# Attention values: a wide matmul over both parts of the weights, and a sum in two halves

## The chip, the cores and the metric

The kernel runs on one core of one Trainium2 chip. The metric is device microseconds from the start to the end of one execution; lower is better. TensorE multiplies, ScalarE and VectorE do the element-wise work, GpSimd helps at a few places, and the SP queue issues the weight transfers.

## The reference, cut to what matters

Two transformer stacks run one after the other on 256 tokens of width 1024, in fp32. Two of their layers have attention: the second layer of the first stack (called layer 0 of the attention in the kernel) and the layer of the second stack (layer 1). The part that the change touches is the projection to queries, keys and values:

```
z = h @ w_in
qkv = z[..., :3 * ATT_W].reshape(bsz, s, 3, H_ATT, HEAD_DIM).transpose(2, 0, 3, 1, 4)
q, k, v = qkv[0], qkv[1], qkv[2]
...
xn = rmsnorm_2(h, g_attn[i])
proj = xn @ w_in[i]
sb_q, sb_k, sb_v, d_q, d_k, d_v = jnp.split(proj, offsets, axis=-1)
```

Values are then weighed by softmax probabilities (layer 0: forgetting and block attention; layer 1: differential attention, then stick-breaking attention).

## The kernel before

**Precision.** Every large product is made of three fp32r products: x and the weights are each split into a high part (rounded to fp32r) and a low part (what is left), and high·high, low·high and high·low are summed in PSUM. ScalarE rounds the weights (line 578, `wh`), VectorE or GpSimd subtracts (lines 974 and 516, `wl`).

**Units.** Weights come in units of 1024 columns of 128 partitions, four to a quad, each in a slot of a ring of four (`raw`, `wh`, `wl`, each `[P, RING, SLOT]`). A semaphore `lo_ready[s]` tells TensorE that a slot is split. Queries and keys are made with the weights as the stationary operand and x moving (`unit`, lines 1556 to 1558): 24 matmuls of 256 columns. Values are wanted with tokens on the partitions, so there x is stationary and the weights move (`value_unit`, lines 1679 to 1682).

**The projection of a layer.** It has 24 units, u = 0 to 23, in four groups g of six: query and key of one head pair (u%6 = 0, 1), two units that together hold the values of two pairs (2, 3), and query and key of the next pair (4, 5). The head pairs are taken in turns j = 0 to 9; in turn j TensorE works through units 3j, 3j+1 and 3j+2, and between them `scores(j-1)`, `turn(j-1)` (transposes of the probabilities, line 1767) and `weigh(j-2)` (probabilities times values, lines 1792 and 1794). The order is written out by hand for each engine. An engine takes its instructions in order.

**Banks.** The projection has three PSUM banks (0 to 2). `bank_free(u)` holds TensorE until the unit that last used the bank has been read. Queries and keys are read by VectorE (`read_out`, line 1295, semaphore `bank_read`), values by ScalarE (`read_values`, line 823, semaphore `values_read`). Both values halves (tokens 0 to 127 and 128 to 255) share one bank. Scores are in banks 3 and 4, transposed probabilities in banks 5 and 6 (`turned_banks`), the output in bank 7.

**VectorE's turn j** is, in order: `logits(j-1)` (line 1319), `read_out(3j)`, the split of unit 3j+3 (`split_next(3j-1)`), `normalise(j-1)` (lines 1334 to 1351), `read_out(3j+1)` in the first two turns, the split of unit 3j+4, the low part of an output, later turns' `read_out(3j+1)`, the split of unit 3j+5 and `read_out(3j+2)`. In layer 1 the first turn also has one reciprocal (line 1465), after which GpSimd scales h (lines 561 and 562) beside the next turns. ScalarE's turn has the softmax exponentials (line 798), the rounding of a unit (line 578), then in odd turns `read_values`.

## Time and profile before

| | |
|---|---|
| time, three runs | 906.71 us median (906.47 to 907.17) |
| the profiled execution | 907.1 us, span 905.4 us |
| TensorE matmuls | 898.6 us busy, 99% of the span |
| VectorE, ScalarE, GpSimd busy | 670.1, 572.1, 243.6 us |
| granted TensorE clock | 0.999 |
| chain that ended last | TensorE 95%, VectorE 2%, ScalarE 1% |

The span runs from the first to the last instruction of the profiled execution; 1.7 us of its time lie outside the span. A matmul's busy time overlaps that of the next, so that how fast TensorE goes is read from the starts of successive matmuls and not from their durations.

### The profile page before, as it was taken

To read this page: it belongs to the slowest core of one execution; us is meant where nothing else is said; L and a number is where in the kernel's file an instruction comes from. 1 tells how busy PE (TensorE), PEld (TensorE's weight loads), DVE (VectorE), ACT (ScalarE), POOL (GpSimd) and SP (SyncE) were. 2 spreads that over 40 slices of the span, in tenths; PEclk is the share of its full clock that TensorE was granted. 3 is DMA by queue.
4 is the path that set the end of the run, shared out by engine and by line. 5 is a ranking of instruction groups with operands and counts; after the bars stand their busy time and mean duration, and the time that the engine had idled before them with its cause. 6 is when DMAs were issued, how large, how long until landed. Compare 5 with 4: busy or idle time off the path is not lost.

```text
span 905.4 us, 18274 instructions
## 1 busy us (share of the span) xinstructions
PE 898.6 (99%) x6022; PEld 814.0 (90%) x6022; DVE 670.1 (74%) x1353; ACT 572.1 (63%) x996; POOL 243.6 (27%) x130
## 2 busy tenths in 40 slices
PE   9999999999999999999999999999999999999997
PEld 8999888888898999988888888999998888888897
DVE  8987887786657756678777866788667766686566
ACT  7456776774445556577666644667658877774453
POOL 0421444420000002044443000070104988850000
PEclk9999999999999999999999999999999999999999
DMA  8545677677534434456666654444335655576521
GB/s 307 196 167 163 210 236 238 210 225 268 173 130 140 139 129 153 162 167 210 231 193 212 230 190 147 127 154 141 119 122 179 211 190 192 192 236 208 185 96 47
DMA packets 47193, 163.51 MB, mean 181 GB/s; under 512 B 5234, under 2 KB 10098, under 8 KB 47141
## 3 DMA queue, kind: packets, MB, share of 16 engines
q1 hardware_dynamic: 42336, 158.12, 53.5%
q10 hardware_dynamic: 4805, 4.70, 1.6%
q8 instruction: 32, 0.52, 0.3%
q14 instruction: 20, 0.16, 0.1%
HBM read 161.71 MB, written 3.44 MB: 182 GB/s over the span
## 4 chain that ended last, share of the span: by engine, by line
PE 95%; DVE 2%; ACT 1%; issue 1%; DVEq 0%
PE psum L1532 41%; PE psum L1533 20%; PE psum L1556 7%; PE psum L1557 7%; PE psum L1558 7%; PE psum L1679 2%; PE psum L1681 2%; PE psum L1682 2%; PE psum L1792 1%; PE psum L1894 1%; PE psum L1767 1%; PE psum L1731 1%; PE psum L1729 1%; ACT wh L578 1%; PE psum L1905 0%
## 5 line engine op out<-in xcount | busy, mean ns | idle before, releaser
L578 ACT ACTIVATE wh<-raw 128x1024 fp32r<-128x1024 f32 (+2 forms) x266 | 297.1, 1119 | 116.4 <-PE psum L1533 80.6
L1532 PE MATMUL psum<-xs,wh 128*128 128x512 f32 x1056 | 367.2, 394 | 0.0
L516 POOL TENSOR_TENSOR wl<-raw,wh 128x1024 fp32r<-128x1024 f32 (+1 forms) x86 | 209.5, 2440 | 450.7 <-ACT wh L578 449.3
L1533 PE MATMUL psum<-xs,wl 128*128 128x256 f32 x1056 | 292.7, 277 | 0.0
L974 DVE TENSOR_TENSOR wl<-raw,wh 128x1024 fp32r<-128x1024 f32 (+2 forms) x180 | 241.3, 1345 | 52.3 <-ACT wh L578 52.0
L1532 PEld LDWEIGHTS psum<-xs,wh 128*128 128x128 f32 x1056 | 198.0, 188 | 45.9
L1533 PEld LDWEIGHTS psum<-xs,wl 128*128 128x128 f32 x1056 | 198.3, 188 | 0.1
L1532 PE MATMUL psum<-ys,wh 128*128 128x512 f32 x528 | 183.2, 394 | 0.0
L1533 PE MATMUL psum<-ys,wl 128*128 128x256 f32 x528 | 146.3, 277 | 0.0
L1556 PE MATMUL psum<-xs,wh 128*128 128x256 f32 x416 | 120.3, 289 | 0.0
L1532 PEld LDWEIGHTS psum<-ys,wh 128*128 128x128 f32 x528 | 99.0, 188 | 23.0
L1558 PE MATMUL psum<-xs,wl 128*128 128x256 f32 x416 | 117.6, 283 | 0.0
L1557 PE MATMUL psum<-xs,wh 128*128 128x256 f32 x416 | 117.6, 283 | 0.0
L1031 DVE SCALAR_TENSOR_TENSOR psum<-work,vec,psum 128x256 f32<-128x256 f32 x184 | 88.7, 482 | 23.7 <-ACT psum L732 23.3
L1533 PEld LDWEIGHTS psum<-ys,wl 128*128 128x128 f32 x528 | 99.1, 188 | 0.0
L1023 DVE TENSOR_TENSOR psum<-psum,work 128x256 f32<-128x256 f32 x132 | 56.6, 429 | 40.8 <-ACT work L729 40.6
L729 ACT ACTIVATE work<-psum 128x256 f32<-128x256 f32 x132 | 50.4, 382 | 51.1 <-PE psum L1533 50.8
L1556 PEld LDWEIGHTS psum<-xs,wh 128*128 128x128 f32 x416 | 79.6, 191 | 1.6 <-issue 1.4
L1557 PEld LDWEIGHTS psum<-xs,wh 128*128 128x128 f32 x416 | 79.7, 192 | 0.1
L1558 PEld LDWEIGHTS psum<-xs,wl 128*128 128x128 f32 x416 | 79.6, 191 | 0.0
L732 ACT ACTIVATE psum<-work,vec 128x256 f32<-128x256 f32 x88 | 50.1, 569 | 36.7 <-DVE work L1014 33.7
L1014 DVE TENSOR_TENSOR work<-psum,rstd 128x256 f32<-128x256 f32 x100 | 42.1, 421 | 5.2
(239 smaller groups left out, 1230.3 us busy)
## 6 DMA issues: line engine op xcount, KB each, us to landing
raw<-in_up SPq DMA_DIRECT2D x132, 512.0 KB, 3.3
raw<-in_down SPq DMA_DIRECT2D x48, 704.0 KB, 4.2
raw<-in_qkv SPq DMA_DIRECT2D x48, 512.0 KB, 3.3
raw<-in_out SPq DMA_DIRECT2D x16, 512.0 KB, 3.4
raw<-in_even_in SPq DMA_DIRECT2D x12, 512.0 KB, 3.6
raw<-in_ple SPq DMA_DIRECT2D x8, 640.0 KB, 3.8
raw<-in_even_out SPq DMA_DIRECT2D x8, 512.0 KB, 3.6
raw<-in_even_in SPq DMA_DIRECT2D x8, 256.0 KB, 5.2
```

Source lines behind the costliest of these rows:

```text
L516: nc.gpsimd.tensor_tensor(low, raw[:, s, 0:tiles * P], high.bitcast(f32), ALU.subtract)\
L578: nc.scalar.activation(split_weights(q, s, tiles * P)[0], raw[:, s, 0:tiles * P], ACT.Copy).then_inc(hi_ready, 1)
L729: nc.scalar.activation(high_sums[:, s % 2, :], proj[:, s, 0:SEQ], ACT.Copy).then_inc(high_copied, 1)
L732: nc.scalar.activation(target, padded[:, 2:2 + SEQ], ACT.Identity, bias=column(bias_name, chunk), scale=column(taps, chunk + 2 * chunks)). ...
L974: nc.vector.tensor_tensor(low, raw[:, s, 0:tiles * P], high.bitcast(f32), ALU.subtract).then_inc(lo_ready[s], 1)
L1023: return nc.vector.tensor_tensor(proj[:, s, 0:SEQ], proj[:, s, SEQ:2 * SEQ], high_sums[:, s % 2, :], ALU.add)
L1031: return nc.vector.scalar_tensor_tensor(out_ap, padded[:, k:k + SEQ], column(taps, chunk + k * chunks), out_ap, ALU.mult, ALU.add)
L1532: nc.tensor.matmul(bank, wh[:, s, w], inputs(t), start=first, stop=False)
L1533: done = nc.tensor.matmul(bank[:, SEQ:2 * SEQ], wl[:, s, w], inputs(t)[:, 0, :], start=False, stop=last)
L1556: nc.tensor.matmul(bank, high_w[:, w], high, start=first, stop=False)
L1557: nc.tensor.matmul(bank, high_w[:, w], low, start=False, stop=False)
L1558: done = nc.tensor.matmul(bank, low_w[:, w], high, start=False, stop=last)
```

## The change

A value unit now takes, for each tile of x and each half of the tokens, two matmuls in place of three. The first has x's high part stationary and moves both parts of the weights, 2 times 256 columns, into a whole bank of 512: the first 256 columns collect high·high, the second 256 high·low. The second matmul adds low·high to the first 256 columns. For this `wh` and `wl` become the two planes of one tensor `both_parts`, and each token half has a bank of its own: banks 2 and 5 in group 0, banks 1 and 2 in later groups.

The two column halves of a bank must be added. ScalarE scales the first half into `qkv` as before, now with `values_scaled` after each token half; VectorE then multiplies the second half by the same factor and adds it (`add_values`, two SCALAR_TENSOR_TENSOR), and gives `values_read`. Since banks are shared otherwise, the waits of TensorE change: in groups 1 to 3 unit 6g+5 waits for `values_read` of its own group (before: for the read of unit 6g+1), unit 6g+2 waits for the read of unit 6g (before: 6g-1), unit 6g+4 for that of unit 6g+1 (before: 6g). In group 0 the transposes `turn(0)` wait for `values_read` (before: `token_ready`).

```diff
@@ memory and banks @@
-        wh = sb("wh", [P, RING, SLOT], f32r)
-        wl = sb("wl", [P, RING, SLOT], f32r)
+        both_parts = sb("both_parts", [P, 2, RING, SLOT], f32r)
+        wh, wl = both_parts[:, 0, :, :], both_parts[:, 1, :, :]
...
+        def unit_of_bank(u):
+            return (2, 0, None, None, 0, 1)[u % 6] if u >= 6 else u if u < 2 else u - 4
 
         def qkv_bank(u):
-            return psum[:, bank_use(u) % QKV_BANKS, 0:2 * SEQ if is_value(u) else SEQ]
+            return psum[:, unit_of_bank(u), 0:SEQ]
+
+        def value_bank(u, b):
+            return psum[:, (2, 5)[b] if u < 6 else 1 + b, :]
@@ ScalarE @@
                     for b in range(2):
-                        last = nc.scalar.activation(qkv[:, u - 1:u + 3:3, b * P:(b + 1) * P],
-                                                    qkv_bank(u)[:, b * SEQ:(b + 1) * SEQ].rearrange("p (c d) -> p c d", c=2),
-                                                    ACT.Identity, scale=token_rstd[:, b:b + 1])
-                    last.then_inc(values_read, 1)
+                        nc.scalar.activation(qkv[:, u - 1:u + 3:3, b * P:(b + 1) * P],
+                                             value_bank(u, b)[:, 0:SEQ].rearrange("p (c d) -> p c d", c=2),
+                                             ACT.Identity, scale=token_rstd[:, b:b + 1]).then_inc(values_scaled, 1)
@@ VectorE @@
+                def add_values(g):
+                    u = 6 * g + 3
+                    for b in range(2):
+                        dve.wait_ge(values_scaled, 2 * (PAIRS // 2 * layer + g) + b + 1)
+                        at = qkv[:, u - 1:u + 3:3, b * P:(b + 1) * P]
+                        last = nc.vector.scalar_tensor_tensor(at, value_bank(u, b)[:, SEQ:2 * SEQ].rearrange("p (c d) -> p c d", c=2),
+                                                              token_rstd[:, b:b + 1], at, ALU.mult, ALU.add)
+                    last.then_inc(values_read, 1)
...
                     if turn and not late:
                         normalise(j - 1)
+                    if j < PAIRS and j % 2 == 1:
+                        add_values(j // 2)
@@ TensorE @@
                 def bank_free(u):
-                    use = bank_use(u) - QKV_BANKS
-                    if use < 0:
+                    g, at = divmod(u, 6)
+                    if g == 0 and at == 2:
                         pe.wait_ge(bank_read, q0 * RING)
-                    elif use % 5 == 2:
-                        pe.wait_ge(values_read, PAIRS // 2 * layer + use // 5 + 1)
-                    else:
-                        pe.wait_ge(bank_read, q0 * RING + reads_to(use))
+                    elif g and at == 0 or at == 5 and g:
+                        pe.wait_ge(values_read, PAIRS // 2 * layer + g + (at == 5))
+                    elif at != 3:
+                        pe.wait_ge(bank_read, q0 * RING + ((0, 4 * g - 1, 4 * g + 1, 0, 4 * g + 2)[at] if g else at - 3))
...
                         for b in range(2):
-                            tokens, sums = slice(b * P, (b + 1) * P), bank[:, b * SEQ:(b + 1) * SEQ]
-                            nc.tensor.matmul(sums, xs[:, t, 0, tokens], wh[:, s, w], start=first and i == 0 and b == 0, stop=False,
+                            tokens, bank = slice(b * P, (b + 1) * P), value_bank(u, b)
+                            nc.tensor.matmul(bank, xs[:, t, 0, tokens], both_parts[:, :, s, w], start=first and i == 0, stop=False,
                                              skip_group_check=True)
-                            nc.tensor.matmul(sums, xs[:, t, 0, tokens], wl[:, s, w], start=False, stop=False, skip_group_check=True)
-                            last = nc.tensor.matmul(sums, xs[:, t, 1, tokens], wh[:, s, w], start=False,
+                            last = nc.tensor.matmul(bank[:, 0:SEQ], xs[:, t, 1, tokens], wh[:, s, w], start=False,
                                                     stop=not first and i == DC // 2 - 1, skip_group_check=True)
...
                         if n == 0:
-                            pe.wait_ge(token_ready, layer + 1)
+                            pe.wait_ge(values_read, PAIRS // 2 * layer + 1)
```

TensorE's rows of layer 1, group 1, before: the end of unit 9 (values), `weigh(1)`, the first matmuls of unit 10, and the first of unit 11.

```order
L1679 MATMUL psum<-wh,xs 128x256
L1681 MATMUL psum<-wl,xs 128x256
L1682 MATMUL psum<-wh,xs 128x256
L1792 MATMUL psum<-work,qkv 128x256 [waits values_read,turned_read,diff_mean]
L1794 MATMUL psum<-work,qkv 128x128
L1556 MATMUL psum<-xs,wh 128x256 [waits lo_ready2,bank_read]
...
L1556 MATMUL psum<-xs,wh 128x256 [waits lo_ready3,bank_read]
```

The same place of the change (line numbers of the changed program).

```order
L1693 MATMUL psum<-both_parts,xs 128x512
L1695 MATMUL psum<-both_parts,xs 128x256
L1806 MATMUL psum<-work,qkv 128x256 [waits values_read,turned_read,diff_mean]
L1808 MATMUL psum<-work,qkv 128x128
L1568 MATMUL psum<-xs,both_parts 128x256 [waits lo_ready2,bank_read]
...
L1568 MATMUL psum<-xs,both_parts 128x256 [waits lo_ready3,values_read]
```

Three narrow matmuls have become a wide and a narrow one, and the last row, unit 11, waits for `values_read` where it waited for `bank_read`.

VectorE's rows of the same turn (j = 3 of layer 1), before: the end of `normalise(2)`, the split of unit 13, the low part of an output, `read_out(10)`.

```order
L1351 SCALAR_TENSOR_TENSOR work<-work,row_inv 128x128
L1351 SCALAR_TENSOR_TENSOR work<-work,row_inv 128x256
L974 TENSOR_TENSOR wl<-raw,wh 128x1024
L1018 TENSOR_TENSOR ys<-diff,ys 128x256
L1295 TENSOR_TENSOR qkv<-psum,rstd 128x256
```

And now:

```order
L1361 SCALAR_TENSOR_TENSOR work<-work,row_inv 128x128
L1361 SCALAR_TENSOR_TENSOR work<-work,row_inv 128x256
L1303 SCALAR_TENSOR_TENSOR qkv<-psum,token_rstd,qkv 128x2x128 x2
L974 TENSOR_TENSOR both_parts<-raw,both_parts 128x1024
L1018 TENSOR_TENSOR ys<-diff,ys 128x256
L1295 TENSOR_TENSOR qkv<-psum,rstd 128x256
```

The two additions (L1303) stand behind `normalise` and ahead of the split, and everything behind them in VectorE's queue moves back by two instructions.

## Rows read from the trace of the kernel before

**Rows 1.** The page, busy time by engine: us, share of span, instructions.

```profile
PE 898.6 (99%) x6022; PEld 814.0 (90%) x6022; DVE 670.1 (74%) x1353; ACT 572.1 (63%) x996; POOL 243.6 (27%) x130
```

**Rows 2.** Waits of TensorE (total us, times, longest): two lines, the longer.

```profile
PE psum L1894 <- DVE ones L1035: 1.1, 1, 1.1
...
```

**Rows 3.** Groups by line and shape, TensorE: count, busy us, mean ns.

```profile
L1679 PE MATMUL psum<-wh,xs 128*128 128x256 f32 x128 | 37.2, 291 | 0.0
```

**Rows 4.** Timeline, TensorE, a value unit: start us, us (22 starts apart).

```profile
269.02 0.28 PE L1681 MATMUL psum<-wl,xs 128*128 128x256 f32 x1
...
271.64 0.28 PE L1682 MATMUL psum<-wh,xs 128*128 128x256 f32 x1
```

**Rows 5.** Timeline, TensorE, feed-forward: wide and narrow matmuls by turns (12 pairs).

```profile
239.84 0.39 PE L1532 MATMUL psum<-ys,wh 128*128 128x512 f32 x1
240.07 0.27 PE L1533 MATMUL psum<-ys,wl 128*128 128x256 f32 x1
...
244.00 0.39 PE L1532 MATMUL psum<-ys,wh 128*128 128x512 f32 x1
```

**Rows 6.** Groups by line and shape, VectorE: the nearest instructions to the additions.

```profile
L1031 DVE SCALAR_TENSOR_TENSOR psum<-work,vec,psum 128x256 f32<-128x256 f32 x184 | 88.7, 482 | 23.7 <-ACT psum L732 23.3
L1295 DVE TENSOR_TENSOR qkv<-psum,rstd 128x256 f32<-128x256 f32 x32 | 13.2, 417 | 16.5 <-PE psum L1558 16.3
```

**Rows 7.** Timeline, layer 0, group 0: the reading of the values and `turn(0)`.

```profile
282.15 0.81 ACT L823 ACTIVATE qkv<-psum,token_rstd 128x256 f32<-128x256 f32 x2
283.90 0.82 PE L1767 MATMUL psum<-ident,work 128*128 128x128 f32 x6
```

**Rows 8.** Timeline, layer 0, group 1: the reading of the values and unit 11.

```profile
302.28 0.81 ACT L823 ACTIVATE qkv<-psum,token_rstd 128x256 f32<-128x256 f32 x2
303.77 0.39 PE L1556 MATMUL psum<-xs,wh 128*128 128x256 f32 x1
```

**Rows 9.** Timeline, layer 1, group 0: VectorE, and `turn(0)` on TensorE.

```profile
582.24 0.75 DVE L1351 SCALAR_TENSOR_TENSOR work<-work,row_inv 128x128 f32<-128x128 f32 x2
582.90 0.42 DVE L1295 TENSOR_TENSOR qkv<-psum,rstd 128x256 f32<-128x256 f32 x1
583.88 0.49 PE L1767 MATMUL psum<-ident,work 128*128 128x128 f32 x3
587.50 0.36 DVE L1295 TENSOR_TENSOR qkv<-psum,rstd 128x256 f32<-128x256 f32 x1
588.15 0.29 DVE L1319 CUSTOM_DVE_ANT_0 work<-psum,bias 128x128 f32<-128x128 f32 x1 [0.29 <-PE psum L1731]
```

**Rows 10.** Timeline, layer 1, turn 2: `normalise(1)` to `scores(2)`.

```profile
591.28 0.18 DVE L1334 RECIPROCAL row_inv<-row_sum 128x4 f32<-128x4 f32 x1 [0.78 <-ACT work L798]
593.42 1.76 DVE L974 TENSOR_TENSOR wl<-raw,wh 128x1024 fp32r<-128x1024 f32 x1
594.08 1.89 POOL L561 TENSOR_SCALAR h<-h,vec 128x256 f32<-128x256 f32 x1
595.10 0.41 DVE L1295 TENSOR_TENSOR qkv<-psum,rstd 128x256 f32<-128x256 f32 x1
595.57 0.49 PE L1729 MATMUL psum<-qkv 64*128 64x128 f32 x4
```

**Rows 11.** Timeline, layer 1, turn 3: VectorE, and the start of unit 11.

```profile
600.36 1.76 DVE L974 TENSOR_TENSOR wl<-raw,wh 128x1024 fp32r<-128x1024 f32 x1
600.86 0.81 ACT L823 ACTIVATE qkv<-psum,token_rstd 128x256 f32<-128x256 f32 x2
602.92 0.28 PE L1556 MATMUL psum<-xs,wh 128*128 128x256 f32 x1
603.20 1.34 DVE L1351 SCALAR_TENSOR_TENSOR work<-work,row_inv 128x128 f32<-128x128 f32 x2
604.46 1.22 DVE L974 TENSOR_TENSOR wl<-raw,wh 128x1024 fp32r<-128x1024 f32 x1
605.59 0.95 DVE L1018 TENSOR_TENSOR ys<-diff,ys 128x256 fp32r<-128x256 f32 x1
```

More of the change, by code:

```diff
@@ L247, in build_program @@
         proj, aux = psum[:, 0:RING, :], psum[:, RING:2 * RING, :]
-        QKV_BANKS = 3
         score_banks, turned_banks = psum[:, 3:5, :], psum[:, 5:7, :]
@@ L260, in is_value @@
             return u % 6 in (2, 3)
-        def bank_use(u):
-            return 5 * (u // 6) + (0, 1, 2, 2, 3, 4)[u % 6]
-        def reads_to(use):
-            return 4 * (use // 5) + (1, 2, 2, 3, 4)[use % 5]
+        def unit_of_bank(u):
+            return (2, 0, None, None, 0, 1)[u % 6] if u >= 6 else u if u < 2 else u - 4
         def qkv_bank(u):
-            return psum[:, bank_use(u) % QKV_BANKS, 0:2 * SEQ if is_value(u) else SEQ]
+            return psum[:, unit_of_bank(u), 0:SEQ]
+        def value_bank(u, b):
+            return psum[:, (2, 5)[b] if u < 6 else 1 + b, :]
         def scores_behind(kind, n):
@@ L362, in build_program @@
         turned_read = sem("turned_read")
+        values_scaled = sem("values_scaled")
         values_read = sem("values_read")
@@ L1671, in value_unit @@
                 def value_unit(u, tiles):
-                    s, bank, first = u % RING, qkv_bank(u), u % 6 == 2
+                    s, first = u % RING, u % 6 == 2
                     pe.wait_ge(lo_ready[s], q0 + u // RING + 1)
```

## The prediction

> **What bounds the kernel now.** I read the page first: TensorE is busy 99% of the span [rows 1]. Busy time of overlapping matmuls proves little, so I went to its waits: the longest is 1.1 us, at the very start [rows 2], and there is none inside either attention layer. TensorE runs from one matmul to the next through all 24 units of both projections. Two things follow: a shorter instruction stream on TensorE is worth its full length, and so is a new wait. The timeline gives the pace. In a value unit 22 successive starts take 2.62 us, 0.119 us per narrow matmul [rows 4]. In the feed-forward layers a 512-column and a 256-column matmul alternate, and 12 pairs take 4.16 us, 0.347 us a pair [rows 5].
>
> **What the change removes.** Line 1679 stands 128 times in the trace, so there are 128 triples [rows 3]. A triple costs 3 x 0.119 = 0.357 us, a pair 0.347 us; the gain is 0.0106 us x 128 = 1.36 us, which is 0.085 us for a value unit (8 triples) and 0.68 us for a layer. The columns moved are the same 768; only one start is saved. The moving operand of the new wide matmul is two runs of 256 columns in place of one run of 512, which no row shows; I take it at the price of the wide one, the bound below nothing is excluded by the equal column count, and the bound above is the triple's own price, that is, no gain.
>
> **What it adds.** Sixteen additions on VectorE, two a group. The nearest row is a SCALAR_TENSOR_TENSOR with a PSUM input, 482 ns; a plain read of a projection bank has 417 ns [rows 6]. Instructions overlap by 0.08 us (the one at 582.90 ends at 583.32, its successor in the queue started before that), so a pair occupies VectorE's queue for 0.80 us and is finished after 0.88 us. TensorE started 0.06 us after VectorE's release (595.51 to 595.57) [rows 10]. VectorE as a whole has room for 7 us more (74% busy [rows 1]); what counts is where the pair stands, since it stands behind `normalise`, and `values_read` now comes after it. I go through the places where TensorE asks for it.
>
> *Layer 0, group 0.* The values are scaled by 282.96; the second addition ends about 0.5 us later, 283.5. `turn(0)` stood at 283.90 and comes 0.17 us sooner (two value units), at 283.73 [rows 7]. No wait.
>
> *Layer 0, group 1.* Scaling ended at 303.09, with 0.17 us of gain 302.92, the second addition at 303.45, TensorE free to go at 303.5. Unit 11 stood at 303.77 and would come at 303.43 after four value units [rows 8]. A wait of 0.1 us. Behind the additions in VectorE's queue stands also the copy that `turn(2)` waits for (`f_ready`); I allow another 0.1 us. In groups 2 and 3 unit 6g+5 comes later against VectorE's turn, and I count nothing. Layer 0: -0.68 + 0.2 = -0.5 us.
>
> *Layer 1, group 0.* VectorE is through with `normalise(0)` at 582.90. The pair lasts to 583.78, and `turn(0)`, due at 583.71, starts at 583.84: 0.13 us, which eats this group's gain [rows 9]. More important is the queue behind: `read_out(4)`, two splits, `read_out(5)`, the reciprocal and `read_out(6)` follow without a gap, all 0.80 us later. The only slack is 0.29 us ahead of `logits(1)` at 588.15 [rows 9]. So `logits(1)` is 0.51 us late. The exponentials wait for it, and VectorE for them (0.78 us of idle at 591.28 is that wait), so the lateness is not absorbed. From there the queue is full until `read_out(7)`, which ends at 595.51, and `scores(2)` starts at 595.57 [rows 10]: TensorE is already held there by VectorE. It becomes 596.08, TensorE 0.51 us behind.
>
> *Layer 1, group 1.* This is the term that decides. Unit 11 started at 602.92 and had nothing to wait for. Its new wait is for additions that stand behind `normalise(2)`, and VectorE is only through with that at 604.46 in the trace of before [rows 11]: 1.5 us after unit 11 had begun. ScalarE's part is done long before (601.67). With the 0.51 us the additions start at 604.97, end at 605.85, and unit 11 starts at 605.91, 2.99 us later than before. This difference holds all gains and delays of the layer up to there; the wait itself would be 2.6 us (unit 11 arrives at 602.92 + 0.51 - 0.085 = 603.35). Queued behind unit 11 on TensorE are everything else of the layer, and nothing later gives it back, since TensorE had no idle time to lose.
>
> *Layer 1, groups 2 and 3.* Four value units give 0.34 us. These turns have stick-breaking, without `normalise` ahead of the additions, so the pair comes early in the turn; for unit 17 I allow 0.05 us. Layer 1: +2.99 - 0.34 + 0.05 = +2.7 us.
>
> The splits move back with the queue. Each makes a unit that TensorE uses a quad later, three to four units at 2.9 us, against 0.8 us; nothing. The loads that SP issues on `lo_ready` are another quad ahead. The new waits of units 6g+2 and 6g+4 are for reads finished a unit earlier.
>
> **The sum.** -0.5 + 2.7 = +2.2 us. The profiled execution took 907.1 us and becomes 909.3; it stands 0.4 us above the median of the runs, so against 906.71 us I predict 908.9 us.
>
> **Where a rule of the Trainium skill bears.** In turn 3 GpSimd works beside VectorE, and some VectorE instructions are longer there: the split has 1.76 us at 600.36 and 1.22 us at 604.46, and the low part of an output 0.95 us [rows 11] against 0.42 us for a like read in rows 6. The bounds of the pair are thus 0.88 us and 2 x 0.95 = 1.9 us, the latter giving 909.9 us. I take the lower, since the nearest in operands, `read_out(7)` with one PSUM and one SBUF input, took 0.41 us entirely beside a GpSimd instruction (594.08 to 595.97) [rows 10]. The Trainium skill (SBUF — State Buffer, SBUF: two separate sides) says that a VectorE instruction and one of GpSimd shut each other out when VectorE's is in a two-port mode or has two SBUF inputs. By that rule an addition with a PSUM input is never held up and the sum stays 908.9 us; the trace agrees, with its 0.41 us.
>
> **The rivals.**
> 1. *The additions are slowed by GpSimd*: 909.9 us, as above. For it: the slow instructions around 604 us. Against: the 0.41 us. Chance 0.08.
> 2. *TensorE's clock falls in the 2.6 us of idle*: the page has 2.4 GHz granted throughout, and no gap of such length. One unit (2.9 us) at 1.2 GHz would cost 2.9 us more, 911.8 us. Chance 0.05.
> 3. *Not slower: VectorE reaches the additions sooner.* The place is layer 1, turns 2 and 3. Three instructions there are stretched: two splits (593.42 and 600.36) by 0.54 us each, the last pair of `normalise(2)` by 0.59 us (1.34 against 0.75) [rows 9, 10, 11]. GpSimd's work starts after the reciprocal, which is now 0.80 us later, so it meets other instructions. If all three came out short, 1.67 us of the wait go and the time is 907.2 us. From 0.4 us on the change is no longer told from none. Against it: the GpSimd work is the same in amount and would fall on neighbours. Chance 0.24.
> 4. *Faster*: the wide matmul costs less than in rows 5, or the wait at unit 11 vanishes. The second alone gives 906.71 - 1.36 + 0.4 = 905.8 us, still within 0.2%; so this needs the first, against the row's 0.23 us start to start. Chance 0.03, time below 904.9 us. The Trainium skill (TensorE: Matmul & The Clock Gate, Back-to-back issue gap) gives 131 ns as the sustained spacing at 512 columns. By that rule a pair would have 0.25 us, the gain would be 0.107 x 128 = 13.7 us and the time about 896.6 us; this trace disagrees, with 0.23 us in every wide matmul of rows 5.
>
> **How the numbers follow.** The forecast has chance 0.60. A change under 0.2% (1.8 us, 904.9 to 908.5) can't be told from none here. Slower is the forecast with rivals 1 and 2, 0.73; same is rival 3, 0.24; faster rival 4, 0.03. The range runs from rival 3's full size, 907.2 us, to somewhat over rival 1's, 910.6 us, and leaves out rivals 2 and 4 and the tails, under 2 in 10.
>
> **What would show it.** In the timeline of after: value units of 8 x 0.347 = 2.8 us; the pair of additions 0.8 to 0.9 us; `scores(2)` of layer 1 about half a microsecond later against the layer's start; a gap of some 2.6 us ahead of unit 11 of layer 1 in TensorE's rows, put down to VectorE's additions; no such gap at units 5, 17 or 23, and at most 0.2 us at layer 0's unit 11. The prediction is wrong if unit 11's wait is much under 2 us, if a second long wait appears, or if the granted clock falls.

## The result and the profile after

The changed kernel takes 912.62 us (median of six runs, 909.97 to 913.77), the kernel before in the same measurement 906.79 us (906.30 to 907.19). The ratio is 1.006, interval 1.0045 to 1.0074: slower, by 5.8 us. Forecast were 908.9 us and at most 910.6. The profiled execution took 911.2 us with a span of 909.4, against 907.1 and 905.4 before, so 4.1 of the 5.8 us can be looked for in the trace.

The page of the changed kernel: busy times, and the queue that loads instructions (packets, MB, share of 16 engines).

```profile
PE 897.3 (99%) x5894; PEld 805.9 (89%) x5894; DVE 676.5 (74%) x1369; ACT 571.7 (63%) x996; POOL 242.9 (27%) x130
q8 instruction: 31, 0.51, 0.2%
```

TensorE has 128 matmuls less and VectorE 16 instructions more than in [rows 1]; both are as busy as before. That says nothing of 4 us. The waits of TensorE do (total us, times, longest):

```profile
PE psum L1568 <- DVE qkv L1303: 2.3, 1, 2.3
PE psum L1895 <- DMA qkv<-in_rel: 1.4, 1, 1.4
PE psum L1908 <- DVE ones L1035: 1.1, 1, 1.1
PE psum L1742 <- DVE qkv L1295: 0.9, 1, 0.9
```

Before, the 1.1 us at the start was the longest [rows 2]. There are three new ones: a unit of queries or keys (L1568) waits for an addition (L1303), the scores of a pair (L1742) wait for VectorE's `read_out`, and at the very start a matmul waits for a small load. The timelines of the same kernel place the first two: TensorE around 606 us and 596 us, then VectorE around 605 us.

```profile
603.73 0.28 PE L1570 MATMUL psum<-xs,both_parts 128*128 128x256 f32 x1
606.33 0.39 PE L1568 MATMUL psum<-xs,both_parts 128*128 128x256 f32 x1 [2.33 <-DVE qkv L1303]
```

```profile
595.18 0.49 PE L1781 MATMUL psum<-ident,work 128*128 128x128 f32 x3
596.54 0.49 PE L1742 MATMUL psum<-qkv 64*128 64x128 f32 x4 [0.87 <-DVE qkv L1295]
```

```profile
601.33 1.77 DVE L974 TENSOR_TENSOR both_parts<-raw,both_parts 128x1024 fp32r<-128x1024 f32 x1
604.18 1.31 DVE L1361 SCALAR_TENSOR_TENSOR work<-work,row_inv 128x128 f32<-128x128 f32 x2
605.41 0.86 DVE L1303 SCALAR_TENSOR_TENSOR qkv<-psum,token_rstd,qkv 128x256 f32<-128x256 f32 x2
```

The first is unit 11 of layer 1, at 606.33 where it stood at 602.92 [rows 11]. The additions end at 606.27 and TensorE starts 0.06 us later. The long split and `normalise(2)` still stand ahead of the pair, stretched as before.

To see where the 4.0 us of span come from I cut both traces at the same instructions: the matmuls of the statistics ahead of each attention layer, and the last `weigh` of each. For layer 1 these are the rows below, before and then after.

```profile
570.02 0.60 PE L1587 MATMUL psum<-acc,ones 128*128 128x256 f32 x2
667.46 0.39 PE L1794 MATMUL psum<-work,qkv 128*64 128x128 f32 x4
```

```profile
570.21 0.60 PE L1599 MATMUL psum<-acc,ones 128*128 128x256 f32 x2
670.78 0.39 PE L1808 MATMUL psum<-work,qkv 128*64 128x128 f32 x4
```

| stretch, us | before | after | difference |
|---|---|---|---|
| start to layer 0 | 268.46 | 268.94 | +0.48 |
| layer 0 | 96.34 | 96.05 | -0.29 |
| between the layers | 205.22 | 205.22 | 0.00 |
| layer 1 | 97.44 | 100.57 | +3.13 |
| last `weigh` to the first store's issue | 233.14 | 233.13 | -0.01 |
| first store's issue to the end | 4.80 | 5.49 | +0.69 |

So 2.84 us lie in the attention layers, where the sum had 2.2, and 1.2 us at the two ends of the program, where nothing was edited. The last row comes from these rows of the two timelines and the spans (`out` is stored by five transfers; before, then after):

```profile
900.60 2.65 SPq L493 DMA_DIRECT2D out<-h  x5
```

```profile
903.91 2.65 SPq L494 DMA_DIRECT2D out<-h  x5
```

The issue takes the same 2.65 us; it is the transfers that land later. Last the value units: the first and the last matmul of the same unit in TensorE's timeline, before, and then in the changed kernel.

```profile
292.14 0.28 PE L1679 MATMUL psum<-wh,xs 128*128 128x256 f32 x1
...
294.90 0.29 PE L1682 MATMUL psum<-wh,xs 128*128 128x256 f32 x1
```

```profile
292.50 0.40 PE L1693 MATMUL psum<-both_parts,xs 128*128 128x512 f32 x1
292.74 0.28 PE L1695 MATMUL psum<-both_parts,xs 128*128 128x256 f32 x1
...
294.97 0.40 PE L1693 MATMUL psum<-both_parts,xs 128*128 128x512 f32 x1
295.21 0.28 PE L1695 MATMUL psum<-both_parts,xs 128*128 128x256 f32 x1
```

Seven pairs in 2.47 us are 0.353 us a pair, 0.24 of it for the wide matmul. From its first to its last matmul the unit took 2.76 us before and takes 2.71 now, 0.05 us less where the prediction counted 0.085. The starts of all sixteen value units, each with the step to the next instruction, add up to 47.7 us before and 46.9 now. The gain is 0.8 us, not 1.36: about 0.47 in layer 0 and 0.38 in layer 1.

### The profile page after: what moved, and what is told of

Same layout as the page of the kernel before. It is cut to its first block, busy times and chain, and to the rows that moved or that the text cites. A ratio compares the mean times of both kernels' runs of the same rounds, so it can differ in the third digit from the quotient of the medians.

```text
span 909.4 us, 18026 instructions
## 1 busy us (share of the span) xinstructions
PE 897.3 (99%) x5894; PEld 805.9 (89%) x5894; DVE 676.5 (74%) x1369; ACT 571.7 (63%) x996; POOL 242.9 (27%) x130
## 4 chain that ended last, share of the span: by engine, by line
PE 91%; DVE 5%; ACT 2%; issue 1%; DMA 1%; ACTq 0%; DVEq 0%
PE psum L1544 40%; PE psum L1545 20%; PE psum L1568 7%; PE psum L1569 7%; PE psum L1570 7%; PE psum L1693 3%; PE psum L1695 1%; DVE both_parts L974 1%; PE psum L1806 1%; PE psum L1781 1%; ACT both_parts L579 1%; DMA qkv<-in_rel 1%; PE psum L1919 0%; PE psum L1744 0%; PE psum L1920 0%
## 5 line engine op out<-in xcount | busy, mean ns | idle before, releaser
L579 ACT ACTIVATE both_parts<-raw 128x1024 fp32r<-128x1024 f32 (+2 forms) x266 | 297.1, 1119 | 114.4 <-PE psum L1545 80.7
L1544 PE MATMUL psum<-xs,both_parts 128*128 128x512 f32 x1056 | 367.2, 394 | 0.0
L517 POOL TENSOR_TENSOR both_parts<-raw,both_parts 128x1024 fp32r<-128x1024 f32 (+1 forms) x86 | 209.6, 2445 | 455.2 <-ACT both_parts L579 453.8
L1545 PE MATMUL psum<-xs,both_parts 128*128 128x256 f32 x1056 | 293.2, 278 | 0.0
L974 DVE TENSOR_TENSOR both_parts<-raw,both_parts 128x1024 fp32r<-128x1024 f32 (+2 forms) x180 | 241.8, 1348 | 51.6 <-ACT both_parts L579 51.4
L1544 PEld LDWEIGHTS psum<-xs,both_parts 128*128 128x128 f32 x1056 | 198.3, 188 | 45.8
L1545 PEld LDWEIGHTS psum<-xs,both_parts 128*128 128x128 f32 x1056 | 198.4, 188 | 0.1
L1544 PE MATMUL psum<-ys,both_parts 128*128 128x512 f32 x528 | 183.2, 394 | 0.0
L1545 PE MATMUL psum<-ys,both_parts 128*128 128x256 f32 x528 | 146.5, 278 | 0.0
L1568 PE MATMUL psum<-xs,both_parts 128*128 128x256 f32 x416 | 120.6, 290 | 2.3 <-DVE qkv L1303 2.3
L1544 PEld LDWEIGHTS psum<-ys,both_parts 128*128 128x128 f32 x528 | 99.1, 188 | 23.0
L1570 PE MATMUL psum<-xs,both_parts 128*128 128x256 f32 x416 | 117.8, 283 | 0.0
L1569 PE MATMUL psum<-xs,both_parts 128*128 128x256 f32 x416 | 117.7, 283 | 0.0
L1545 PEld LDWEIGHTS psum<-ys,both_parts 128*128 128x128 f32 x528 | 99.2, 188 | 0.0
L1568 PEld LDWEIGHTS psum<-xs,both_parts 128*128 128x128 f32 x416 | 79.7, 192 | 4.2 <-DVE qkv L1303 2.5
L1569 PEld LDWEIGHTS psum<-xs,both_parts 128*128 128x128 f32 x416 | 79.7, 192 | 0.1
L1570 PEld LDWEIGHTS psum<-xs,both_parts 128*128 128x128 f32 x416 | 79.7, 192 | 0.0
L1693 PE MATMUL psum<-both_parts,xs 128*128 128x512 f32 x128 | 46.8, 406 | 0.0
```

The lines of the kernel that those rows point to most:

```text
L517: nc.gpsimd.tensor_tensor(low, raw[:, s, 0:tiles * P], high.bitcast(f32), ALU.subtract)\
L579: nc.scalar.activation(split_weights(q, s, tiles * P)[0], raw[:, s, 0:tiles * P], ACT.Copy).then_inc(hi_ready, 1)
L974: nc.vector.tensor_tensor(low, raw[:, s, 0:tiles * P], high.bitcast(f32), ALU.subtract).then_inc(lo_ready[s], 1)
L1544: nc.tensor.matmul(bank, wh[:, s, w], inputs(t), start=first, stop=False)
L1545: done = nc.tensor.matmul(bank[:, SEQ:2 * SEQ], wl[:, s, w], inputs(t)[:, 0, :], start=False, stop=last)
L1568: nc.tensor.matmul(bank, high_w[:, w], high, start=first, stop=False)
```

## The experiments

Each comparison is of five rounds, with the kernel before beside it on the same chip; the kernels came in four batches, in which the median of before was 906.64 to 906.99 us. "Peel" below means one loop pass on TensorE written out, with the same matmuls executed.

| kernel | median us (range) | ratio, interval |
|---|---|---|
| a0_again | 911.98 (911.69 to 914.16) | 1.0067, 1.0054 to 1.008 |
| a1_spare | 908.82 (908.26 to 911.89) | 1.0028, 1.0017 to 1.0039 |
| a4_fill | 911.47 (911.05 to 911.60) | 1.0053, 1.004 to 1.0066 |
| b2_wait_read10 | 912.93 (912.15 to 914.17) | 1.0067, 1.0054 to 1.008 |
| b3_planes | 906.75 (906.36 to 907.38) | 1.0002, 0.9993 to 1.0011 |
| a3_no_add | 907.71 (907.45 to 909.19) | 1.0013, 1.0004 to 1.0022 |
| a5_narrow | 910.04 (909.22 to 910.45) | 1.0034, 1.0022 to 1.0046 |
| a2_early | 908.01 (907.72 to 910.50) | 1.0019, 1.001 to 1.0028 |
| a8_peel | 910.10 (908.96 to 911.32) | 1.0035, 1.0023 to 1.0047 |
| a9_no_add_peel | 905.92 (905.39 to 906.37) | 0.9989, 0.998 to 0.9999 |
| a7_both | 910.44 (910.32 to 910.68) | 1.004, 1.0026 to 1.0054 |
| b4_late_recip | 909.09 (908.53 to 909.60) | 1.0025, 1.0016 to 1.0034 |
| c1_early_peel | 907.19 (906.45 to 907.87) | 1.0005, 0.9996 to 1.0014 |
| c2_spare_peel | 906.76 (906.21 to 907.70) | 1.0002, 0.9993 to 1.0011 |
| c3_fill_peel | 909.56 (909.33 to 910.13) | 1.0033, 1.0022 to 1.0044 |
| b5_peel | 907.07 (906.13 to 907.36) | 1.0001, 0.9992 to 1.001 |

### First: is it unit 11's wait, and does the clock come into it?

My theory: the wait of unit 11 explains the bulk, and the rest is TensorE's clock falling after it in some executions (the prediction's rival 2). The rival: the rest has nothing to do with unit 11.

**The changed kernel again**, without an edit.

> The changed kernel again, unchanged. The profiled execution of it was 911.2 us with TensorE's last matmul 3.3 us later than before, while other executions read 912 to 914 us at a mean granted clock of 0.995 or 0.996 in place of 0.998. Theory A: the wait of TensorE ahead of unit 11 of layer 1 (2.5 us of idle) lets the granted clock fall behind it in most executions; then runs at 0.998 lie near 910 to 911 us, runs at 0.995 to 0.996 near 912.4 to 914 us, and a profile of such a run shows a stretch at 1.2 GHz ahead of the last microseconds. Theory B: the clock falls only after TensorE's last matmul, and the spread comes from transfers at the start and the end; then the time goes with the first matmul's start and the last store, not with the clock.

It came out at 911.98 us: more than 5 us are reproduced. Together with the six executions of the first measurement there are eleven, each with its time and its mean granted clock on record. Three have 0.998 and took 909.97 to 911.69 us; eight have 0.995 or 0.996 and took 911.85 to 914.16 us. The two profiled executions are of the first kind, and in their traces the clock is at 0.5 only behind TensorE's last matmul. The executions of before that were measured beside the experiments have 0.998 to 1.0.

**Unit 11 of layer 1 in a bank of its own.** Bank 6 is unused there, so nothing has to be waited for; the additions stay.

```diff
+                    elif layer == 1 and u == 11:
+                        pass
...
-                    unit(..., qkv_bank(u), ...)
+                    unit(..., spare_bank[:, 0, :] if layer == 1 and u == 11 else qkv_bank(u), ...)
```

> The changed kernel with unit 11 of layer 1 summed in the spare bank 6 in place of bank 1, so that it has no wait for the values. Theory A: the 2.5 us of idle and every fall of the clock go; median near 908 us (before 906.8, +0.8 of wait ahead of scores(2), some 0.3 of small waits, -1.4 of saved matmuls, and up to 1 us for transfers at the end), and all executions lie within 1 us at a clock of 0.998 to 0.999. Theory B: 2.5 us less than the changed kernel, about 910 us, with the same spread of 4 us.

908.82 us: 3.2 to 3.8 us go with the wait, the largest part. Layer 1 shrinks from 100.57 to 98.09 us, so the trace shows 2.5 of them. But 2.1 us over before (906.67 us in this batch) remain, and only 0.7 of them are layer 1's. One of the seven executions took 911.89 us, at a mean clock of 0.995: there a fall came without the wait at unit 11, and no trace shows where.

**The idle filled**: seven matmuls of ones by ones, which end before the additions do.

```diff
+                    if layer == 1 and j == 3:
+                        for _ in range(FILL):      # FILL = 7
+                            nc.tensor.matmul(spare_bank[:, 0, 0:P], ones[:, :], ones[:, :], start=True, stop=True)
                     qkv_unit(3 * j + 2)
```

> The changed kernel with seven matmuls of ones by ones (128 columns, fp32, about 2.1 us) into the unused bank 6 ahead of unit 11 of layer 1: the wait stays, TensorE is busy in it. Theory A: TensorE's stream is as late as in the changed kernel's profile (3.3 us), but the clock does not fall: all executions near 910.5 to 911.2 us, 1.5 to 2 us under the changed kernel's median. Theory B: no difference from the changed kernel, 912.6 us with the same spread.

The wait is still there (layer 1 again 100.57 us), TensorE's last idle being 0.77 us. The median falls by 0.5 to 1.1 us against the two unfilled measurements, and the spread from 3.8 and 2.5 to 0.55 us. All five executions have a clock of 0.998 or 0.999: what the filling takes away is the longest executions, those with the lower clock.

**Before, with a wait at unit 11** for the read of unit 10, which VectorE makes behind `normalise(2)` and a split. Nothing else is changed.

```diff
+                    if layer == 1 and j == 3:
+                        pe.wait_ge(bank_read, q0 * RING + 7)
                     qkv_unit(3 * j + 2)
```

> The kernel before with one wait more: unit 11 of layer 1 waits for the read of unit 10, which in the trace of before ended at 606.88 us against unit 11's start at 602.92 us, so 4.0 us of idle, nothing else changed. Theory A: 906.8 + 4.0 = 910.8 us and on top of it 1.5 to 2 us in most executions for the clock, 912 to 913 us, clock 0.996. Theory B: 910.8 us and no more, clock as before.

912.93 us. Its profile shows the clock fall that the profiles of the changed kernel don't. The windows of this kernel (length, busy time and count by engine, granted clock, DMA share, GB/s):

```profile
602.00:604.00 2.00, 1.51 (x13) 1.31 (x11) 1.89 (x7) 1.35 (x5) 1.92 (x2) 1.00 0.15 20
604.00:606.00 2.00, 0.00 (x0) 0.00 (x0) 2.00 (x3) 0.67 (x1) 1.92 (x3) 1.00 0.62 242
606.00:608.00 2.00, 0.66 (x3) 0.66 (x4) 2.00 (x4) 0.00 (x0) 0.67 (x1) 0.58 0.34 82
608.00:610.00 2.00, 2.00 (x11) 2.00 (x11) 0.41 (x1) 0.00 (x0) 0.00 (x0) 0.50 0.68 223
610.00:612.00 2.00, 2.00 (x12) 2.00 (x11) 0.00 (x0) 0.00 (x0) 0.00 (x0) 0.50 0.56 219
612.00:614.00 2.00, 2.00 (x13) 1.84 (x12) 0.85 (x2) 1.08 (x2) 0.00 (x0) 0.71 0.00 0
```

No matmul starts on TensorE between 603.23 and 607.34. Where a window's clock is between 1.00 and 0.50 it changed inside: 0.58 puts the fall at 606.3, 0.71 the rise at 613.2. In between it is 0.5, that is 1.2 GHz, and matmuls of 256 columns start 0.21 us apart (607.72 and 607.93) where they start 0.12 us apart at 2.4 GHz. Layer 1 is 6.66 us longer than before: 4.0 of idle, and 2.7 of clock. A wait alone, put into the old kernel, thus costs its own length and 2.7 us of clock besides. That the total is near the change's is chance: this idle time is 1.5 us longer than the change's, and this kernel has 32 packets on the instruction queue.

### Second: what else is in it?

The rest of a1_spare's loss could be the tensor of two planes, the wide matmul, or the additions' place in VectorE's queue.

**Before, with the two planes only**: `wh` and `wl` as planes of `both_parts`, three narrow matmuls as before.

> The kernel before with one edit: wh and wl are the two planes of one tensor. All instructions and waits are those of before. In the profiles of the kernels with both_parts the span ends 5.5 us after the first store's issue and in those without it 4.8 us after. If the tensor's form is the reason, this kernel shows 5.5 us there and a median of 907.4 us; if the 0.7 us belong to something else, 4.8 us and 906.7 us.

No difference (906.75 us): where the weights lie costs nothing.

**The changed kernel without the additions.** The low part of the weights is left out of the values; ScalarE gives `values_read` itself.

```diff
-                    if j < PAIRS and j % 2 == 1:
-                        add_values(j // 2)
```

> The changed kernel without the additions: ScalarE gives values_read itself, so the low part of the weights is left out of the values. Wide matmuls, banks and waits otherwise as changed. If the whole loss comes from the additions' place in VectorE's queue, all waits of TensorE go, its stream in the two attention layers is 1.3 us shorter than before (0.6 to 0.7 us a layer), no execution shows a clock under 0.998, and the median is 905.5 to 906.1 us (with 0.7 us at the end if the stores are slower). If the wide matmul is not worth 0.085 us a value unit, the layers are as long as before.

This has every saving of the change and no cost of VectorE's, and it is still 1.1 us slower than before (906.64 us in this batch). Its layers are 0.47 and 0.55 us shorter than before's (95.87 and 96.89 us), 1.0 us in all, of which the value units are 0.8. So some 2 us are lost outside them.

**The changed kernel with narrow matmuls**: the wide one is made as two, into the same bank.

```diff
-                            nc.tensor.matmul(bank, xs[:, t, 0, tokens], both_parts[:, :, s, w], ...)
+                            nc.tensor.matmul(bank[:, 0:SEQ], xs[:, t, 0, tokens], wh[:, s, w], ...)
+                            nc.tensor.matmul(bank[:, SEQ:2 * SEQ], xs[:, t, 0, tokens], wl[:, s, w], ...)
```

> The changed kernel with the wide matmul undone: high x high and high x low in two 256-column matmuls into the two halves of the bank; additions, banks and waits as changed. A value unit takes 24 x 0.119 = 2.86 us in place of 2.77; layer 0 is 0.6 us longer than in the changed kernel, layer 1 about 0.4 us longer, since units ahead of the wait at unit 11 only shorten the wait. Median 912.4 + 1.0 = 913.4 us, with the clock's spread; the wait at unit 11 shrinks by 0.1 us.

It is *faster* than the changed kernel, 910.04 against 912 to 912.6 us, with 128 matmuls more. Two things differ in its trace. The transfers at the ends are as before (first store's issue to end 4.8 us). And `scores(2)` doesn't wait. There VectorE's order is the same, but GpSimd, which scales h beside it, stands a little otherwise. The timelines of VectorE and GpSimd in turn 2, first of the changed kernel, then of a5_narrow:

```profile
592.46 1.24 DVE L1358 TENSOR_SCALAR work<-work,row_inv 128x128 f32<-128x128 f32 x2
594.40 1.75 DVE L974 TENSOR_TENSOR both_parts<-raw,both_parts 128x1024 fp32r<-128x1024 f32 x1
```

```profile
594.09 0.98 POOL L563 TENSOR_TENSOR h<-h,mid_rstd 128x256 f32<-128x256 f32 x1
595.05 1.89 POOL L562 TENSOR_SCALAR h<-h,vec 128x256 f32<-128x256 f32 x1
```

```profile
593.36 1.21 DVE L974 TENSOR_TENSOR both_parts<-raw,both_parts 128x1024 fp32r<-128x1024 f32 x1
```

```profile
593.42 1.73 POOL L563 TENSOR_TENSOR h<-h,mid_rstd 128x256 f32<-128x256 f32 x1
```

The same split takes 1.75 us when it starts inside a GpSimd instruction and 1.21 us when it starts 0.06 us ahead of one, and then it is GpSimd's that is stretched, from 0.98 to 1.73 us. This agrees with the Trainium skill (SBUF — State Buffer, SBUF: two separate sides): a VectorE instruction with two SBUF inputs and one of GpSimd shut each other out, and whoever is first goes first. `scores(2)` has its 0.9 us of wait, or none, by some tens of nanoseconds. The additions, with their PSUM input, took 0.86 us beside GpSimd's work, as forecast.

This kernel's profile also has a clock fall, after a shorter idle time: no matmul starts between 602.20 and 604.46, and by the windows the granted clock is 0.5 from 605.6 to 609.0. Windows and two rows of a5_narrow's TensorE:

```profile
604.00:606.00 2.00, 1.54 (x11) 1.54 (x12) 2.00 (x5) 0.00 (x0) 2.00 (x2) 0.90 0.03 12
606.00:608.00 2.00, 2.00 (x12) 2.00 (x11) 1.48 (x3) 0.00 (x0) 1.92 (x2) 0.50 0.51 193
608.00:610.00 2.00, 2.00 (x13) 1.90 (x13) 0.85 (x2) 0.86 (x1) 0.07 (x1) 0.74 0.77 256
```

```profile
604.46 0.39 PE L1568 MATMUL psum<-xs,both_parts 128*128 128x256 f32 x1 [1.98 <-DVE qkv L1303]
...
606.07 0.41 PE L1570 MATMUL psum<-xs,both_parts 128*128 128x256 f32 x1
606.28 0.41 PE L1568 MATMUL psum<-xs,both_parts 128*128 128x256 f32 x1
```

Starts are 0.21 us apart there, 0.12 elsewhere; unit 11 takes 4.4 us where it takes 3.0, which costs 1.4 us.

**The additions earlier**: in layer 1, group 1, ahead of `normalise(2)`.

```diff
+                    early_add = layer == 1 and j == 3
+                    if early_add:
+                        add_values(j // 2)
                     if turn and not late:
                         normalise(j - 1)
-                    if j < PAIRS and j % 2 == 1:
+                    if j < PAIRS and j % 2 == 1 and not early_add:
                         add_values(j // 2)
```

> The changed kernel with the additions of layer 1's group 1 ahead of normalise(2) in place of behind it. In the changed kernel's trace VectorE got to normalise(2) 2.4 us ahead of the additions and ScalarE had scaled by then. Theory: the wait at unit 11 falls from 2.5 us to 0.2 us at most, the clock stays (no execution under 0.998), and the median is near 909.3 us, like the kernel with the spare bank (908.8). If normalise(2), now 0.8 us later, holds up turn(2), some of it comes back there: up to 910 us.

908.01 us, and no wait at unit 11. The order in VectorE's queue is worth 4 us. What remains against before is 1.4 us. In the profiled execution layer 1 is 98.30 us, with the wait of `scores(2)` still in it, and the transfers at the ends are the late ones of the changed kernel. But that execution took 909.12 us, 1.1 us more than the median, and the eleven fall into two groups: six from 907.72 to 908.01 us and five from 908.88 us up. That the lower group is the one without the wait of `scores(2)` fits its 0.9 us, but no trace of that group was kept.

### Third: the ends of the program

Set side by side, the kernels fell into two kinds: those with 31 packets on the instruction queue (after, a0, a1, a2, a3, a4) had their first stores land after 2.7 or 2.8 us and x after 6.4 to 6.7 us; those with 32 (before, b3, a5) 2.1 us and 4.8 to 5.2 us. b2 stood between (32 packets, 2.1 us, but x in 6.4). The theory: it is TensorE's shorter program text, 128 matmuls fewer in unrolled value units, that somehow moves the transfers. The rival: the wide matmul or the additions do it. The test makes the text longer again, with no instruction more executed; the same edit is tried on three others and on before.

```diff
-                each_quad(pe, 1, quads_of[name], quad)
+                peeled = name in ("up0", "up1")
+                if peeled:
+                    quad(1)
+                each_quad(pe, 2 if peeled else 1, quads_of[name], quad)
```

> The changed kernel with one pass of the loops of up0 and up1 written out on TensorE: the same matmuls in the same order, but the program in memory is again as long as before (128 matmuls and their weight loads more). All six kernels with the wide matmul showed slower first loads of x (6.4 to 6.7 us against 4.8 to 5.2 in before, the narrow form and the planes alone), 31 packets in place of 32 in the instruction queue q8, and first stores of 2.7 us against 2.1. Theory of the program's length: with 32 packets the loads and stores are as before and the median falls by some 2 us, to 910.3 us, like the narrow form (910.0). Rival (the wide matmul itself is the reason): 912.4 us, loads at 6.6 us.

> The kernel without the additions (the low part of the weights is left out of the values), with the same loops written out once. Without the peeling it took 907.7 us though its attention layers were 1.0 us shorter than before. Theory of the program's length: 905.6 to 905.9 us, faster than before by the 1.0 us. Rival: 907.7 us again.

Both fell, to 910.10 us (by 1.9 to 2.5) and 905.92 us (by 1.8 against a3_no_add). The transfers, as the two pages and lists of transfers have them (KB, us to landing), first after, then a8_peel:

```profile
raw<-in_even_in SPq DMA_DIRECT2D x8, 256.0 KB, 7.0
h<-in_x SPq DMA_DIRECT2D x4, 256.0 KB, 6.6
out<-h SPq DMA_DIRECT2D x3, 256.0 KB, 2.7
```

```profile
q8 instruction: 32, 0.52, 0.2%
h<-in_x SPq DMA_DIRECT2D x4, 256.0 KB, 5.2
out<-h SPq DMA_DIRECT2D x3, 256.0 KB, 2.1
```

The attention layers of a8_peel are those of after (layer 1: 100.60 us). In its profile the last transfers end 4.8 us after the first store's issue, 0.7 us sooner, and the small load of the third new wait no longer holds TensorE at the start. Over all profiles of this case the two ends are as follows.

| | start to layer 0 | first store's issue to the end |
|---|---|---|
| 31 packets, seven kernels | 268.9 to 269.5 us, mean 269.2 | 5.5 us in each |
| 32 or 33 packets, eleven kernels | 267.7 to 268.9 us, mean 268.3 | 4.8 us in each |

The end is 0.7 us longer in every profile with 31 packets. The start is 0.9 us longer in the mean, with a scatter of 0.5 and 1.2 us within the two kinds. So the traces show 1.6 us of the 2. The 0.48 us of start in the first table is one draw from this scatter.

Two other kernels of this batch asked whether the VectorE and GpSimd collisions can be removed. The reciprocal (line 1465 of before) after which GpSimd starts is moved to the end of turn 3; `diff_t`, which lies in the buffer that it reads, goes to `mid_acc`: a7_both is a1_spare with that, b4_late_recip is before with it.

```diff
-        diff_t = bias[:, HEADS, :]
+        diff_t = mid_acc[:, :]
...
-                    if layer == 1 and j == 1:
+                    if layer == 1 and j == 3:
...
```

> The changed kernel with unit 11 of layer 1 in the spare bank and the reciprocal of layer 1 (1.74 us on VectorE, after which GpSimd scales h) moved from the end of turn 1 to the end of turn 3; its old scratch tile is not shared any more. Theory: VectorE's queue in turns 1 to 3 is shorter by 1.74 us and free of GpSimd's collisions, so that the wait of 0.9 us at scores(2) goes as well: no wait of TensorE in layer 1 over 0.2 us, layer 1 of 96.9 us from its statistics to its last weighing (97.4 before), median 907.8 us, 2.1 us of it for loads and stores as in the other wide kernels. Rival: the delay only moves to turns 3 and 4, and the layer is 98 us as with the spare bank alone (908.8 us).

> The kernel before with only that reciprocal moved to the end of turn 3. In before, TensorE was held 0.18 us at scores(2) by VectorE and by nothing else. Expected: 906.5 us, 0.2 us less than before, with splits of 1.2 us in turns 2 and 3 in place of 1.76.

Both are misses: 910.44 and 909.09 us, 1.6 and 2.1 us *slower* than the same kernel without the move. GpSimd's scaling of h went to turns 4 and 5 (607.83 to 624.86 us in b4_late_recip), and TensorE had waits there and behind; how each of them came about wasn't followed. The waits of b4_late_recip on TensorE inside layer 1, where before has none:

```profile
PE psum L1717 <- ACT work L810: 1.2, 1, 1.2
PE psum L1767 <- DVE work L1351: 0.4, 1, 0.4
```

### Fourth: the causes combined

If the three causes add up, the change with no wait at unit 11 and the longer text is as fast as before, and filling the idle gains in the longer text too.

> The changed kernel with both causes undone: the additions of layer 1's group 1 ahead of normalise(2), and one pass of the loops of up0 and up1 written out on TensorE. If the causes add, 908.0 - 2.0 = 906.0 us, 0.7 to 1.0 us less than before. If they don't, over 907 us.

> The changed kernel with unit 11 of layer 1 in the spare bank, and the loops written out likewise. 908.8 - 2.0 = 906.8 us, like before: 0.9 us of wait at scores(2) against 1.0 us of shorter value units.

> The changed kernel with seven matmuls of ones in the wait at unit 11, and the loops written out likewise. If the fall of the clock behind that wait costs time, this kernel is faster than the changed kernel with the loops written out (910.1 us, 908.96 to 911.32) and lies within 0.6 us: 911.5 - 2.0 = 909.5 us. If not, 910.1 us with the same spread of 2.4 us.

> The kernel before with the same loops written out: TensorE's program is 256 instructions longer than before (33 packets in q8), no matmul more is executed. If only a program under some length makes the loads slow, 906.7 us; if each length has loads of its own, another time, with first loads of x off from 4.8 to 5.2 us.

c2_spare_peel took 906.76 us, 2.1 less than a1_spare and level with before. Part of that is luck: in its profile `scores(2)` has no wait, and layer 1 is 0.9 us shorter than a1_spare's, which the longer text was not meant to do. c3_fill_peel took 909.56 us, 1.9 less than a4_fill, spread 0.8 us against a8_peel's 2.4. b5_peel took 907.07 us, no change: the kernel before has nothing to gain from a longer text, it already has its 32 packets (33 then). c1_early_peel was a miss in size: 0.8 us below a2_early, where I had expected some 2. Its profile (906.68 us) has no wait at `scores(2)` either, while its median of 907.19 is half a microsecond above it; so the two medians may stand for executions with and without that wait, and the 0.8 us says little of the text. That isn't settled. No kernel that computes everything beats before; a9_no_add_peel, 1 us below it, leaves the low part of the weights out of the values.

## Why the prediction was wrong in size and right in direction

*The deciding term held.* Unit 11's wait was forecast at 2.6 us, behind `normalise(2)`, and is 2.5 us (603.73 + 0.12 to 606.33); taking it away gives 3.2 to 3.8 us back (a1_spare), moving the additions ahead of `normalise` 4 us (a2_early). The pair of additions was forecast at 0.88 us and takes 0.86; rival 1 is out. No such gap at units 5, 17 and 23.

*The attention layers*: forecast +2.2 us, measured +2.84 in the profiles. Two terms are off. The gain of the value units was mis-sized: 0.085 us a unit from the feed-forward's pairs, 0.05 in fact, so 0.8 us in all where I counted 1.36. The price of a triple came from 22 starts at 0.119 us and that of a pair from other operands; side by side the unit shows the smaller gain. Layer 0 gained 0.29 instead of 0.5 us, 0.47 less the 0.2 of waits that the sum allowed. And `scores(2)` of layer 1 starts 1.36 us behind its predecessor, 0.60 in before, where I had expected 0.51 us more: 0.25 us over. `logits(1)` was 0.41 us late, as good as forecast, but the two instructions of line 1358 in `normalise(1)` then ran beside a GpSimd instruction and took 1.24 us, 0.85 in before. Rival 3 named this mechanism with the other sign; a5_narrow, c1_early_peel and c2_spare_peel have no such wait, which shows that it can go that way, by chance of some tens of nanoseconds.

*The step that failed* is the sum: "the profiled execution took 907.1 us and becomes 909.3". It let nothing happen outside the two attention layers. With 128 matmuls fewer in the program text the transfers at both ends land later. Making the text longer again without executing more took off about 2 us in the three pairs of kernels where the attention layers of both profiles are alike to 0.3 us (1.9 to 2.5, 1.8, 1.9); the two others (2.1 and 0.8 us) are mixed with the wait of `scores(2)`. Against b5_peel, a8_peel is 3.0 us slower, which is the attention layers' 2.84 with little to spare. That the program's text is the cause, and nothing that it executes, is shown; whether it is its length as such or where the code comes to lie, and by which way it reaches the transfers, is not.

*The second step that failed: rival 2 was given 0.05 and left out of the range*. Its ground was that the page showed 2.4 GHz throughout, though the same sentence says that the page had no gap of such length; so it could say nothing. The granted clock falls to 1.2 GHz after the wait in a5_narrow's profile (1.4 us lost) and in b2's (2.7 us). The two profiles of the changed kernel don't show it inside the layer, but its executions spread over 3.8 us, and the fill matmuls narrow that to 0.55. In the median this is 0.5 to 1.1 us (a4_fill, with a8_peel and c3_fill_peel giving 0.5). The long executions are the ones with the lower mean clock: 911.85 to 914.16 us at 0.995 or 0.996, 909.97 to 911.69 at 0.998. A drop of 0.002 over 909 us is, by my estimate, 3.6 us at half the clock, like the 3.4 us of a5_narrow. That their clock falls behind unit 11's wait is inferred from a4_fill and not seen in a trace of them; one execution of a1_spare had a fall without that wait.

Together: 2.84 + 2.0 + 0.5 to 1.1 = 5.3 to 5.9 us, measured 5.8. The last two terms are differences of medians between neighbouring kernels, so they had to come near the total; what checks the sum is that c3_fill_peel, with neither of them, is 2.83 us above before in its own batch (906.73), and the layers' traces say 2.84.

## What to carry to other kernels

When TensorE never waits, ask of each new wait what stands ahead of the releasing instruction in its engine's queue: two additions, 0.86 us together, cost 3 us and more because they stood behind `normalise`, and 4 us came back when one pair was put ahead. A wait of 2 us or more on a busy TensorE is to be priced with a possible stretch at half the clock behind it (here 1.4 and 2.7 us in two profiles, none in three others), even where the old profile shows full clock everywhere. Compare the ends of the program too, loads and stores, when an edit changes the program's length; and take the prices of the old and the new matmuls from the same place.

## What the runs showed of the hardware

- Program text that is shorter by 128 matmuls, 31 instead of 32 packets of instructions, had x land after 6.4 to 6.8 us instead of 4.8 to 5.9 (6.4 in b2_wait_read10), and the first stores after 2.7 or 2.8 instead of 2.1 us; in all about 2 us of execution, of which the traces show 1.6 in the mean. Making the text longer did nothing to a program that has 32 packets already (b5_peel).
- TensorE's granted clock was 0.5 for 3.4 us in the execution with 2 us of idle (a5_narrow) and for 6.8 us in the one with 4 us (b2_wait_read10), and the first stretch began 1.1 us after the matmuls had come back, the second 1.0 us before. The profiles of after, a0_again and a8_peel, with 2.3 us of idle, have no such stretch.
- A matmul of 512 columns whose moving operand lies in two runs of 256 is followed after 0.24 us, 0.23 us with a single run.
- A split on VectorE took 1.21 us started 0.06 us ahead of a GpSimd instruction, 1.75 us started inside one; two additions with a PSUM input took 0.86 us beside GpSimd's work and 0.87 us without it (583.09 us).
